# A decoder layer with mLSTM heads and a conv group on one core: convolution taps packed closer in head 1, two steps reordered, gate rows moved to PSUM

## What is computed

```
x += 1/2 * post_norm(SwiGLU_1(pre_norm(x)))
p  = pre_norm(x) @ w_in        # q, k, v, o gate (4 heads x 256) | glu a, b (1024) | i, f gate (per head)
mLSTM: C_t = f_t C_{t-1} + i_t k_t v_t^T, n_t = f_t n_{t-1} + i_t k_t
       h_t = o_t * (q_t C_t) / max(|n_t.q_t|, exp(-m_t))     # running-max stabiliser m_t
conv:  GLU -> causal depthwise convolution of width 31 -> LayerNorm over channels -> swish
x += post_norm(concat[heads, conv] @ w_out)
x += 1/2 * post_norm(SwiGLU_2(pre_norm(x)))
```

## Time and profile before

| | |
|---|---|
| median of 3 executions | 2163.35 us (2163.24 to 2163.86) |
| the profiled execution | 2164.5 us, of which span 2162.8 us |
| TensorE busy | 2151.5 us, 99% |
| VectorE, ScalarE, GpSimd busy | 994.5, 896.5, 959.5 us (46%, 41%, 44%) |
| granted TensorE clock, mean | 1.000 |
| HBM traffic | 174 GB/s over the span |

### The profile page before, as it was taken

The page is one execution under the profiler, slowest core; times in us unless marked ns, Lnnn a source line. Parts: engine busy times, 40 slices in busy tenths (PEclk is TensorE's granted clock), DMA queues, the critical chain, the costliest instruction groups (busy, mean ns, idle before and its releaser), DMA issues.

```text
span 2162.8 us, 41838 instructions
## 1 busy us (share of the span) xinstructions
PE 2151.5 (99%) x16304; PEld 2140.3 (99%) x16304; DVE 994.5 (46%) x1399; ACT 896.5 (41%) x1164; POOL 959.5 (44%) x561
## 2 busy tenths in 40 slices
PE   9999999999999999999999999999999999999998
PEld 9999999999999999999999999999999999999998
DVE  6533332223343324978769738534332223333322
ACT  6433333333333335544345446433433333333443
POOL 1444443344444444465756332444443334444444
PEclk9999999999999999999999999999999999999999
DMA  6454555554545554556656554555555545554653
GB/s 248 164 171 159 168 167 170 162 165 162 172 156 172 164 169 147 206 189 220 236 193 225 187 165 140 171 166 167 163 166 167 172 157 167 164 173 156 210 167 125
DMA packets 103308, 376.63 MB, mean 174 GB/s; under 512 B 11540, under 2 KB 14612, under 8 KB 102200
## 3 DMA queue, kind: packets, MB, share of 16 engines
q1 hardware_dynamic: 97344, 349.00, 49.2%
q10 hardware_dynamic: 5752, 26.37, 3.4%
q0 software_dynamic: 128, 0.07, 0.0%
HBM read 360.21 MB, written 15.18 MB: 174 GB/s over the span
## 4 chain that ended last, share of the span: by engine, by line
PE 97%; DVE 1%; POOL 1%; ACT 1%; issue 0%; POOLq 0%; ACTq 0%; DVEq 0%
PE bank L463 31%; PE bank L461 31%; PE bank L462 30%; PE bank L803 1%; PE bank L805 1%; PE bank L804 1%; PE bank L724 0%; PE bank L667 0%; PE bank L685 0%; PE bank L524 0%; DVE wlo L1273 0%; POOL wlo L1790 0%; PE bank L708 0%; POOL y L2000 0%; PE bank L656 0%
## 5 line engine op out<-in xcount | busy, mean ns | idle before, releaser
L1790 POOL TENSOR_TENSOR wlo<-raw,whi 128x1024 fp32r<-128x1024 f32 x330 | 794.3, 2408 | 853.4 <-ACT whi L874 758.4
L461 PE MATMUL bank<-xh,whi 128*128 128x288 f32 x3569 | 1058.9, 297 | 0.1
L462 PE MATMUL bank<-xl,whi 128*128 128x288 f32 x3569 | 1054.4, 295 | 0.0
L463 PE MATMUL bank<-xh,wlo 128*128 128x288 f32 x3569 | 1053.2, 295 | 0.0
L874 ACT ACTIVATE whi<-raw 128x1024 fp32r<-128x1024 f32 x652 | 687.4, 1056 | 603.1 <-PE bank L463 571.6
L1273 DVE TENSOR_TENSOR wlo<-raw,whi 128x1024 fp32r<-128x1024 f32 x324 | 467.7, 1445 | 772.1 <-ACT whi L874 770.8
L461 PEld LDWEIGHTS bank<-xh,whi 128*128 128x128 f32 x3569 | 673.1, 189 | 3.1 <-issue 2.2
L463 PEld LDWEIGHTS bank<-xh,wlo 128*128 128x128 f32 x3569 | 672.0, 188 | 0.0
L462 PEld LDWEIGHTS bank<-xl,whi 128*128 128x128 f32 x3569 | 670.9, 188 | 0.2
L463 PE MATMUL bank<-hh,wlo 128*128 128x288 f32 x1408 | 417.4, 296 | 0.0
L461 PE MATMUL bank<-hh,whi 128*128 128x288 f32 x1408 | 416.1, 296 | 0.0
(11 more groups left out here) (260 smaller groups left out, 1089.6 us busy)
## 6 DMA issues: line engine op xcount, KB each, us to landing
raw<-stream SPq DMA_DIRECT2D x654, 512.0 KB, 3.6
C<-c_in ACTq DMA_DIRECT2D x4, 2048.0 KB, 9.3
cs_out<-C ACTq DMA_DIRECT2D x4, 2048.0 KB, 7.9
late<-kvt ACTq DMA_DIRECT2D x4, 512.0 KB, 4.4
late_kv<-late ACTq DMA_DIRECT2D x1, 2048.0 KB, 12.3
bc<-row_copy ACTq DMA_DIRECT2D x4, 448.0 KB, 8.5
conv_out<-upad ACTq DMA_DIRECT2D x4, 302.0 KB, 7.1
y_out<-x_res SPq DMA_DIRECT2D x4, 288.0 KB, 4.1
```

The source lines that it names most:

```text
L461: pe.matmul(out, wh, mov_hi[:, k, :], start=first, stop=False)
L462: pe.matmul(out, wh, mov_lo[:, k, :], start=False, stop=False)
L463: return pe.matmul(out, wl, mov_hi[:, k, :], start=False, stop=last)
L1790: pool.tensor_tensor(wlo[:, g % SLOTS, :], raw[:, g % SLOTS, :], whi[:, g % SLOTS, :].bitcast(F32), ALU.subtract).then_inc(lo_ready[g % SL ...
```

## The change

Four edits. Head 1's taps are done four pairs a piece instead of three, so its decode part comes at piece 38 instead of 41. Head 3's scores stand behind chunk 3 of their piece instead of chunk 1. From piece 94 on, VectorE does the layer norm's part of a piece behind the heads' parts. And the gate chain's rows `raw_f`, `raw_i`, `log_f`, `b_run` and `bm_dec` lie in PSUM banks 4, 5 and 7; head 0's tile k1 moves from bank 4 to bank 7 and waits there for `gates_read` (the gate sums have been read) instead of for the norm's root.

```diff
-TAP_PAIRS = (4, 3, 3, 4)
+TAP_PAIRS = (4, 4, 3, 4)
...
-SPARE_BANK = {4: 5, 5: 6, 6: 7, 7: 4, EARLY_T: 5, tile_of(0, "k0"): 6, tile_of(0, "k1"): 4,
+SPARE_BANK = {4: 5, 5: 6, 6: 7, 7: 4, EARLY_T: 5, tile_of(0, "k0"): 6, tile_of(0, "k1"): 7,
...
-        raw_f, raw_i, log_f, b_run, bm_row = (place(name, [H, PADT], F32, c_at + (5 + k) * pad_bytes)
-                                              for k, name in enumerate(("raw_f", "raw_i", "log_f", "b_run", "bm_row")))
...
-                    if (k, j) == (13, 1 if h else 5):
+                    if (k, j) == (13, (5, 1, 1, 3)[h]):
                         scores(h)
...
                 if T == tile_of(0, "k1"):
-                    pe.wait_ge(norm_sd, 3)
+                    pe.wait_ge(gates_read, 1)
...
-                act.activation(log_f[:, 0:TOK], g_e, ACT.Ln, bias=ones[0:H, 0:1]).then_inc(ln_ready, 1)
+                act.activation(bank[4][0:H, 0:TOK], g_e, ACT.Ln, bias=ones[0:H, 0:1]).then_inc(ln_ready, 1)
...
-            gates = bank[7]
-            rf, ri, lf, br = raw_f[:, 0:TOK], raw_i[:, 0:TOK], log_f[:, 0:TOK], b_run[:, :]
-            bm_dec = bm_row[:, 0:NS].rearrange("h (b t) -> h b t", b=NB)
+            gates, raw_f, raw_i = bank[7], bank[4][0:H, 0:TOK], bank[7][0:H, 0:TOK]
+            log_f, b_run = bank[4][0:H, 0:TOK], bank[tile_bank(EARLY_T)][0:H, 0:PADT]
+            bm_dec = bank[4][0:H, 0:NS].rearrange("h (b t) -> h b t", b=NB)
             dve.wait_ge(gates_done, 1)
-            link(dve.tensor_tensor(rf, gates[NS:NS + H, 0:TOK], rstd[NS:NS + H, :], ALU.mult))
-            dve.tensor_scalar(g_f, rf, gv[:, 1:2], None, ALU.add).then_inc(gf_ready, 1)
-            link(dve.tensor_tensor(ri, gates[0:H, 0:TOK], rstd[0:H, :], ALU.mult))
+            link(dve.tensor_tensor(raw_f, gates[NS:NS + H, 0:TOK], rstd[NS:NS + H, :], ALU.mult))
+            dve.tensor_scalar(g_f, raw_f, gv[:, 1:2], None, ALU.add).then_inc(gf_ready, 1)
+            link(dve.tensor_tensor(raw_i, raw_i, rstd[0:H, :], ALU.mult))
             for k in range(2):
-                dve.tensor_scalar(padded(igp, k), compact(ri, k), gv[:, 0:1], None, ALU.add)
+                last = dve.tensor_scalar(padded(igp, k), compact(raw_i, k), gv[:, 0:1], None, ALU.add)
+            last.then_inc(gates_read, 1)
...
             link(last)
-            dve.tensor_tensor_scan(br, one[:, :], lfb[:, :], 0.0, ALU.mult, ALU.add)
+            dve.wait_ge(tile_evicted, EARLY_T + 1)
+            dve.tensor_tensor_scan(b_run, one[:, :], lfb[:, :], 0.0, ALU.mult, ALU.add)
...
                     if h:
                         dve.wait_ge(cu_evicted, NB * h)
-                    else:
-                        dve.wait_ge(tile_evicted, tile_of(0, "k1") + 1)
...
             for p in range(MIX_FROM, MIX + 8):
                 if p % 2 == 0 and 8 < p <= MIX:
                     evict(p)
-                if p >= MIX - 8:
+                if MIX - 8 <= p < MIX:
                     ln_part(p)
                 for h in range(H):
                     head_part(h, p - KEYS_AT[h])
                     gate_part(h, p - GATE_O_AT[h])
                     conv_part(h, p - CONV_AT[h])
+                if p >= MIX:
+                    ln_part(p)
                 split_lo(HEAD_P + p + LOOK)
```

More of the change, by code:

```diff
@@ L235, in hybrid_layer_kernel @@
         mrun = place("mrun", [H, PADT], F32, c_at + 4 * pad_bytes)
-        raw_f, raw_i, log_f, b_run, bm_row = (place(name, [H, PADT], F32, c_at + (5 + k) * pad_bytes)
-                                              for k, name in enumerate(("raw_f", "raw_i", "log_f", "b_run", "bm_row")))
-        assert 10 * pad_bytes <= 4 * NB * DC * DH
         cpr = place("cpr", [P, DC, DH])
@@ L299, in hybrid_layer_kernel @@
         sel_zero, sel_ready = sem("sel_zero"), sem("sel_ready")
-        gates_part, gates_kept, gates_done = sem("gates_part"), sem("gates_kept"), sem("gates_done")
+        gates_part, gates_kept, gates_done, gates_read = (sem("gates_part"), sem("gates_kept"), sem("gates_done"),
+                                                          sem("gates_read"))
         hi_ready = sem("hi_ready")
@@ L1526, in _ @@
                     last = dve.scalar_tensor_tensor(out=padded(row, k), in0=compact(g_f, k), scalar=0.0,
-                                                    in1=compact(lf, k), op0=ALU.min, op1=ALU.subtract)
+                                                    in1=compact(log_f, k), op0=ALU.min, op1=ALU.subtract)
             link(last)
-            dve.tensor_tensor_scan(br, one[:, :], lfb[:, :], 0.0, ALU.mult, ALU.add)
+            dve.wait_ge(tile_evicted, EARLY_T + 1)
+            dve.tensor_tensor_scan(b_run, one[:, :], lfb[:, :], 0.0, ALU.mult, ALU.add)
             link(dve.tensor_tensor_scan(mrun[:, :], lfm[:, :], igp[:, :], 0.0, ALU.add, ALU.max))
             for k in range(2):
-                dve.tensor_tensor(compact(rows[:, R_BM:R_BM + TOK], k), padded(br, k), padded(mrun, k), ALU.subtract)
-                last = dve.tensor_tensor(compact(rowc, k), padded(igp, k), padded(br, k), ALU.subtract)
-            link(dve.tensor_tensor(bm_dec, padded(br, 1), padded(mrun, 1), ALU.subtract))
+                dve.tensor_tensor(compact(rows[:, R_BM:R_BM + TOK], k), padded(b_run, k), padded(mrun, k), ALU.subtract)
+                last = dve.tensor_tensor(compact(rowc, k), padded(igp, k), padded(b_run, k), ALU.subtract)
+            link(dve.tensor_tensor(bm_dec, padded(b_run, 1), padded(mrun, 1), ALU.subtract))
             dve.tensor_tensor(g_arg[:, 0:NS].rearrange("h (b t) -> h b t", b=NB), compact(rowc, 1),
```

## The result

The changed kernel takes 2167.93 us (2166.79 to 2168.91, 13 runs) where the kernel before takes 2163.28 (2163.09 to 2164.16, 13 runs): a ratio of 1.002, 95% interval 1.0013 to 1.0028. That is 4.65 us or 0.21% slower, just over the 0.2% that the prediction took as the least to be told from no change; the interval leaves no change out. The profiled execution took 2167.7 us (span 2166.0).

A forecast was written before the change was run, and what follows sets the result against it. TensorE, busy 99% of the span, was taken as the bound, with at most 3.2 us to win. Terms +4.8 - 0.3 - 0.5 + 0 + 1.5 = +5.5 us gave 2168.9 us, range 2164.8 to 2171.5.

The forecast's parts named there:

- slower by over 0.2%: Whole kernel: predicted outcome of a time above 2167.7 us, given a chance of 0.64.
- The taps, +5.6: Head 1 on VectorE: 14 taps moved ahead of v1's eviction at 0.40 us each delay it by 5.6 us.
- the second subtraction: VectorE in head 1, 1.19 us at 984.49 before: might meet GpSimd again or miss it; no change taken.
- The collision at piece 34, +1.6: VectorE's low split of piece 34 meets GpSimd's split and takes 3.0 us instead of 1.41: 1.6 us more.
- Given back at head 1's scores, -2.4: Head 1's scores: q1's eviction comes before the scores are due, so TensorE's 2.4 us wait goes.
- Head 3's scores and the query's sum, -0.3 and -0.5: Head 3: TensorE's waits of 0.3 us at the scores and 0.5 us for the query's sum go.
- Gate rows in PSUM, 0: Gate chain and head 0's k1: no gain and no new wait; bounds 0 and +0.9 us, 0 taken.
- The clock, +1.5: TensorE behind the new gap at head 1's transposes: granted clock may fall, costing 1.5 us; bounds 0 and 2.0.
- the upper end of 2.0: Upper bound of the clock's cost: 18 warming matmuls at the start's slower pace, 18 x 0.109 = 2.0 us.
- the clock holds: Rival: the gap comes at head 1 but the clock holds; +4.0 us, 2167.4, or +2.4 without collision; chance 0.34.
- the taps are taken in: Rival: VectorE finds room for the 14 taps in head 1, v1's eviction stays near 995.4; -3.2 us, 2160.2; chance 0.08.
- ScalarE falls behind: Rival: ScalarE, held at v1's copy, is late with high splits for piece 42; +9 us, 2172.4; chance 0.08.

The follow-up runs named there:

- e1: The changed kernel with head 1's taps put back to three pairs a piece, the other three edits kept: 2161.90 us, 1.29 below the kernel before.
- e2: The kernel before with head 1's taps at four pairs a piece and nothing else: 2170.26 us, 7.07 above the kernel before.
- e5: e3 with GpSimd's two additions of head 1's conv output to the layer norm's sum moved from piece 39 to 42: 2163.32 us, ratio to before 0.9999.
- e11: The changed kernel once more, nothing edited, for a second profile: 2169.18 us in one run.
- e8: The kernel before once more, nothing edited, for a second profile: 2163.03 us in one run.
- e7: The kernel before with head 3's scores two chunks later and the query's sum ahead of the layer norm's part, nothing else: 2162.14 us, 1.36 below before.
- e6: The kernel before with the gate chain's rows in PSUM and head 0's k1 in bank 7, nothing else: 2163.13 us, ratio 0.9999.
- e4: The changed kernel with 20 warming matmuls ahead of TensorE's wait at head 1's transposes: 2166.21 us, 3.02 above the kernel before.
- e3: The changed kernel with head 1's v0 and v1 evictions moved on VectorE from pieces 36 and 38 to 35, ahead of its taps: 2163.23 us, ratio to before 1.0002.

## Why the prediction was right, and where its terms were off

The forecast of 2168.9 us was 1 us above the median, its direction and mechanism are those of the traces, and 0.21% lies at the edge of its "slower by over 0.2%". But the closeness is in part luck. The collision was put 1.6 us too high, 1.2 us too much was given back at head 1's scores, and 0.55 us too little in head 3, so a good part of the errors cancels. The bound of the clock's term was too narrow.

**The taps, +5.6: right.** The eviction of v1 and the transposes came 5.5 us later, the 0.37 us taken off. VectorE had no room in this stretch, and ScalarE passed the delay on at once: 1001.69, then 1002.47. e1 and e2 show that this edit is the whole loss. That the 14 taps (5.6 us) come out to the tenth is luck again: VectorE began them 0.8 us less behind TensorE (next paragraph), piece 34's split took 0.2 us less (1.22 for 1.41), and the second subtraction, which the prediction had put at no change, took 1.0 us more beside GpSimd's split (2.15 us at 987.02, for 1.19).

**The collision at piece 34, +1.6: not there.** The step that failed is where the taps start: I let VectorE begin them as far behind TensorE as in the earlier trace rows. In the changed kernel's profile they start at 970.28, while TensorE is 0.37 us later: VectorE is 0.8 us less behind (970.70 - 970.28 + 0.37). The split then came first, and GpSimd's behind it. The 0.8 us hang on which small operation meets GpSimd ahead of the taps. In e5, as in the kernel before, that was the normaliser's `ntmp`, in 2.54 us for two; in the changed kernel's profile it took 0.26 and the next operation on two SBUF inputs, `nns`, 2.14 instead of 0.60, which is 0.74 us less together. The price of the collision was right (e5). The Trainium skill (SBUF — State Buffer, Who interferes with whom) adds that the order of issue, not the kind of operation, decides who is blocked; the pair of starts in e5 (GpSimd first by 0.46 us: 3.00) and in e11 (VectorE first by 0.27: 1.21) agrees with it.

**Given back at head 1's scores, -2.4: mis-sized.** The wait went as predicted, since q1's eviction now waits for TensorE. But 2.4 us was one execution's, and 0.9 is usual (e8). I had the sign of this in hand, as the profiled execution was 1.15 us above its median, and took the waits from it all the same.

**Head 3's scores and the query's sum, -0.3 and -0.5: right waits, too small.** A wait costs more than the idle time that the profile shows for it. Around the query's sum, from the last projection matmul ahead to the first one behind took 2.58 us before (1202.76 to 1205.34) and 1.80 after (1206.69 to 1208.49): 0.78 for an idle of 0.53. At head 3's scores the same comparison gives 0.57 for 0.31. Together they are 1.35 us, and e7 measured 1.36 (in an interval of some 4 us, so the hundredth says nothing). By these 0.25 us or so, the usual 0.9 us at head 1 is worth about 1.2, an estimate. I read them as the refilling of the matmuls' pipeline; no run shows that reason apart.

**Gate rows in PSUM, 0: right.** The last read of the gate sums ended at 890.57 (889.94 + 0.63; 890.2 predicted, with 891.6 for the tile that needs the bank). No wait, and e6 is at no change.

**The clock, +1.5: right as one value, its bound wrong.** It fell behind the gap. e4 gives 1.6 us; the rows of the transposes 1.3. But in e2 and e11 the low clock lasted twice as long and cost some 2.5 us, above the upper end of 2.0. I had taken that end from the number of matmuls at the start of the program, which says nothing of how long a low clock lasts later. The Trainium skill (TensorE: Matmul & The Clock Gate, HAM oscillation) says that idle gaps between groups of matmuls put the array back to half rate; 0.50 in these windows agrees with it; the wait of 2.40 us that left the clock at 1.00 shows that not every gap does.

**The sum** by measured terms: 5.5 + 0 - 1.2 - 1.35 + 0 + 1.6 = 4.55 us, and the medians differ by 4.65. The same terms give e1 against the changed kernel: 5.5 + 1.6 - 1.2 = 5.9, measured 5.94; and e2 with the longer low clock: 5.5 + 2.5 - 1.2 = 6.8, measured 7.07.

**The rivals.** That the clock holds fell (windows, e4). That the taps are taken in fell: 20.00 of 20.00 us busy, v1 late by 5.5. That ScalarE falls behind fell: its next high split starts right behind the copy, at 1002.32, and TensorE has no wait behind the transposes.

Which of the two lengths of the low clock an execution gets, and what decides between them, stays open. So does how often the changed kernel meets the collision at piece 34: it did not in the two executions whose trace there is, nor in those of e2, e3 and e4, which have the same taps; in e5 it did. In both forms `ntmp` begins 0.11 us ahead of GpSimd's split (967.11 and 967.22 in the kernel before, 967.44 and 967.55 in the changed one), so the traces don't show what decides between them.

## What to carry to other kernels

Before work is packed closer on an engine that "is only 46% busy", look at the stretch: where its timeline has no brackets, as here, the packed work moves everything behind it, and a result that another engine takes at once moves with it. Look at a wait of the kernel before in a second execution before it goes into a sum, and add what a wait costs beyond its idle time, here a quarter of a microsecond each. When a step is moved earlier, look for what else is keyed to the same piece (here GpSimd's sum): it will wait in its own queue, in front of something that is needed.

## What was not expected of the hardware

- TensorE's clock fell after a standstill of 2.07 us in e3 (0.50 from 1012 to 1014, eight score matmuls in 2.61 us for 1.47), while a standstill of 2.40 us in the kernel before left it at 1.00.
- The low clock lasted until about 1005.2 us in one execution of the changed kernel and until about 1008.2 in another, behind the same gap of 5.35 us.
- Two SBUF operations of VectorE on 128 x 8 elements took 2.54 us beside GpSimd's split (0.26 in the changed kernel's profile). The place of such a block moves VectorE by 0.7 us and with it, in e5, made a collision ten microseconds later. The two profiles of the kernel before agree on that place (2.54 us both), and so do the two of the changed kernel (0.26); that it differs between executions of one kernel is not shown.
